# V and B of a hybrid decoder layer's input projection as a fourth seven-product pair

## The chip, the cores and the metric

One Trainium2 chip, one core. The metric is the device time of one execution in microseconds (us). TensorE multiplies, ScalarE (ACT) and VectorE (DVE) work on tiles, GpSimd (POOL) does elementwise work beside them, SyncE (SP) and ScalarE issue the transfers.

## The reference, cut to what matters

One layer (D = 1024) over a prompt of 1024 tokens and 8 sample rows, each sample with 4096 past positions in a paged K/V cache. Everything is float32.

```python
h = _rmsnorm(x, g_pre) * (1 + scale[:, None]) + shift[:, None]
p = h @ w_in                                   # 1024 x 4096
hc, bc, cc, gc, q, k, v, ga = jnp.split(p, _split_points(), axis=-1)   # 512 columns each
u = cc * hc
conv_y = sum(conv_w[i] * u_pad[:, i:i + L] for i in range(CONV_WIDTH))
ya = _rmsnorm(bc * conv_y, g_conv) * jax.nn.silu(gc)
o = attend(q, k, v, b_sb).reshape(Bsz, L, ATT_DIM)      # stick-breaking, strictly causal
yb = _rmsnorm(o, g_attn) * jax.nn.silu(ga)
m = jnp.concatenate([ya, yb], axis=-1) @ w_out
y = x + gate[:, None] * _rmsnorm(m, g_post)
# stick-breaking: z = q.k/sqrt(d) + b;  A[t,s] = exp(log_sigmoid(z_ts) + sum_{s<j<t} log_sigmoid(-z_tj))
```

Besides `y`, the outputs are K and V of the prompt (token by token) and of the samples, and the last rows of `u`.

## The kernel before, in words

**Prologue.** The modulation of the layer is computed from `w_ada`, x is normalised and transposed into `hT` (channels on partitions, 8 blocks of 128 channels by 1032 columns: 1024 tokens and 8 samples).

**Groups.** The 512 channels of each of the eight parts of the projection are worked in four groups of 128 channels, two heads each. A group runs through 32 slots `t` and an end. Slots 0 to 7 make Q, K and V; from slot 8 on each slot carries one of 24 attention units `u = t - 8` (`scores`, `clamp`, ScalarE's exponentials, `log_weights`, `turn`, `weights`, `outputs`), and between their steps TensorE works off products for the group's other parts (`pieces_at`). Every engine has its own program with the same slots, in an order written out by hand, and is held to the others by counted semaphores alone. A slot is thus no moment: SP and GpSimd run ahead of TensorE where they can.

**Beside it, the sample rows.** Per group there are two sequences of the sample batch. For each, K pages are loaded in 16 pairs into a ring of four (`load_pair`, SP), GpSimd multiplies a pair by the query (`prod`, two buffers), DVE reduces it (`reduce_pair`), and after two cumulated sums (`cumulate`, `decode_log_weights`) `decode_a` writes the weights into `apad`. V pages are loaded into a second ring and multiplied by TensorE (`value_quad`, eight quads per sequence).

**Seven products.** Two parts (for example Q and K) and the 1024 channels cut in halves make a 2x2 block product. It is done in seven products in place of eight, for chunks of 258 columns and their counterparts 516 columns on: `T1` to `T4` are sums of `hT`'s blocks (made once, DVE's `channel_sums`), `S1`, `S2`, `S4` and an overwritten `a21` are sums of the weight blocks, made by GpSimd in `weight_sum(g, pair, step)`, four steps. `product(i, j)` is product j of chunk i, four matmuls of 258 columns. ScalarE evacuates 1, 5, 6, 2, 4 (`evac_st`: a seed copy inside PSUM, `p5`, `u2`, then the two first outputs), DVE adds 3 and 7 (`product_sum`). Three pairs go this way: Q and K (not in group 0, where `project_qk` makes them directly), the gates GC and GA, and HC and CC.

**V and B.** V is made directly and by tokens (`values(0)`, `values(1)`, `values(2)` for the sample rows): `hT` is the stationary operand, 128 columns of the weight move. B is made directly in three thirds of 344 columns at the end of a group (`project_b`), before and between the last unit's steps. `gating` of a group runs on DVE in slots 0 to 6 of the next group: it multiplies the attention output and the convolution by their gates; in step 2 it takes the sample columns (a scan of two columns and five small copies) and multiplies `hcb` by B (`bcb`). Group 0 to 2 leave their two results in DRAM (`y_parts`).

**Output stage.** `y_parts` is loaded back (SP, after the last group's slots), w_out's eight 128-row slabs go into places that fall free (`wo`), and 16 units of 8 matmuls of 512 columns follow (`out_unit`), the first three in two parts round the last group's gating. Each unit goes through ScalarE and DVE and out.

In DVE's program `log_weights` is line 1239 and its subtraction line 1256, `reduce_pair` line 1226; GpSimd's page product is line 625 and `weight_sum` lines 594 to 608. All matmuls have line 1366 (`mm`), all of ScalarE's operations line 665 (`run`), K and V page loads line 394, w_out's line 400. The orders in question stand in two tables:

```python
EARLY = ((), (1, 5), (2, 6), (3, 7, 11), (4, 15), (12, 16), (13, 17))     # slot: (chunk, product) as two digits
GATING_AT = {0: 0, 1: 1, 2: 2, 4: 3, 5: 4, 6: 5}                          # slot: step
```

## Time and profile before

| | |
|---|---|
| median of 3 runs | 828.58 us (828.44 to 829.12) |
| the profiled execution | 826.34 us |
| its span, first to last instruction | 824.6 us |
| TensorE busy / mean granted clock | 785.9 us / 0.991 |
| DVE, ScalarE, GpSimd busy | 535.7, 352.1, 430.6 us |
| read from and written to HBM | 185 and 12 MB |

A float32 matmul appears in the trace as two records, so 8 records of 258 columns are one product. Matmuls are pipelined and the ends of their records are modelled: the price of a block is the distance from its start to the next block's start. Small transfers and waits that another engine covers cost nothing; what counts is where TensorE stands still.

### The profile page before, as it was taken

To read this page: it belongs to the slowest core of one execution; us is meant where nothing else is said; L and a number is where in the kernel's file an instruction comes from. 1 tells how busy PE (TensorE), PEld (TensorE's weight loads), DVE (VectorE), ACT (ScalarE), POOL (GpSimd) and SP (SyncE) were. 2 spreads that over 40 slices of the span, in tenths; PEclk is the share of its full clock that TensorE was granted. 3 is DMA by queue.
4 is the path that set the end of the run, shared out by engine and by line. 5 is a ranking of instruction groups with operands and counts; after the bars stand their busy time and mean duration, and the time that the engine had idled before them with its cause. 6 is when DMAs were issued, how large, how long until landed. Compare 5 with 4: busy or idle time off the path is not lost.

```text
span 824.6 us, 14401 instructions
## 1 busy us (share of the span) xinstructions
PE 785.9 (95%) x4397; PEld 523.3 (63%) x4397; DVE 535.7 (65%) x728; ACT 352.1 (43%) x729; POOL 430.6 (52%) x230
## 2 busy tenths in 40 slices
PE   0899989999999999999999999999999999999995
PEld 0455866676787676768866767788677665444442
DVE  3576769787585888838758877575787854232344
ACT  7301065775122667811165675122658731212122
POOL 0105895666787567666864685687666630100000
PEclk9989999999999999999999999999999999999998
DMA  8998667577689888776888877868977797554001
GB/s 318 362 348 291 223 225 227 187 240 234 229 260 306 286 255 263 249 248 219 279 290 262 269 238 230 255 234 290 307 253 243 220 360 276 167 188 157 27 27 53
DMA packets 131071, 197.85 MB, mean 240 GB/s; under 512 B 10025, under 2 KB 51030, under 8 KB 130994
## 3 DMA queue, kind: packets, MB, share of 16 engines
q1 hardware_dynamic: 99512, 181.11, 66.0%
q10 hardware_dynamic: 31482, 15.82, 6.9%
q8 instruction: 35, 0.57, 0.3%
q14 instruction: 42, 0.34, 0.2%
HBM read 185.25 MB, written 11.66 MB: 239 GB/s over the span
## 4 chain that ended last, share of the span: by engine, by line
PE 82%; DVE 6%; issue 4%; DMA 3%; POOL 3%; ACT 2%; SPq 1%; ACTq 0%; POOLq 0%; DVEq 0%
PE ps L1366 77%; PE ps L1606 4%; POOL prod L625 2%; DMA xT<-in_x_prompt_dram 2%; DMA ring<-in_w_in_dram 1%; DVE zd L1226 1%; DVE ps L1250 1%; DVE xT L1033 1%; DVE zc L1236 0%; DVE zc L1256 0%; PE ps L1408 0%; ACT tmp L665 0%; PE ps L1638 0%; DVE rows L1070 0%; DMA ring<-in_cache_v_dram 0%
## 5 line engine op out<-in xcount | busy, mean ns | idle before, releaser
L625 POOL TENSOR_TENSOR prod<-ring,qb 128x1024 f32<-128x1024 f32 x128 | 309.3, 2431 | 199.1 <-DVE zd L1226 96.8
L1366 PE MATMUL ps<-hT,wsl 128*128 128x258 f32 (+1 forms) x640 | 174.2, 418 | 0.2 <-DVE zb L1129 0.2
L1226 DVE TENSOR_REDUCE zd<-prod 128x16 f32<-128x1024 f32 x128 | 154.3, 1213 | 21.9 <-POOL prod L625 21.5
L1366 PEld LDWEIGHTS ps<-hT,wsl 128*128 128x128 f32 x640 | 119.1, 190 | 52.8 <-issue 17.3
L1366 PE MATMUL ps<-xT,wS 128*128 128x258 f32 x352 | 92.2, 385 | 0.0
L1366 PE MATMUL ps<-ring,apad 128*32 128x512 f32 x592 | 84.5, 650 | 7.9 <-DMA ring<-in_w_ada_dram 7.2
L1366 PE MATMUL ps<-xT,wsl 128*128 128x258 f32 x352 | 89.6, 386 | 0.0
L1250 DVE TENSOR_TENSOR_SCAN ps<-rise,ps 128x512 f32<-128x512 f32 (+3 forms) x64 | 65.5, 1023 | 34.0 <-ACT ps L665 34.0
L1236 DVE TENSOR_SCALAR zc<-ps,bsb 128x512 f32<-128x512 f32 (+3 forms) x96 | 54.8, 612 | 37.3 <-PE ps L1366 37.0
L665 ACT ACTIVATE rise<-ps,bsh 128x512 f32<-128x512 f32 (+3 forms) x96 | 55.4, 577 | 46.8 <-DVE zc L1236 46.7
L1366 PEld LDWEIGHTS ps<-xT,wsl 128*128 128x128 f32 x352 | 63.0, 190 | 18.6 <-issue 8.0
L665 ACT ACTIVATE av<-ps 128x512 f32<-128x512 f32 (+3 forms) x96 | 46.8, 487 | 60.1 <-PE ps L1606 59.4
L1366 PEld LDWEIGHTS ps<-xT,wS 128*128 128x128 f32 x352 | 62.3, 191 | 15.2 <-issue 8.7
L1366 PEld LDWEIGHTS ps<-wsl,hT 128*128 128x128 f32 (+1 forms) x576 | 63.3, 181 | 7.6 <-issue 6.4
L1366 PE MATMUL ps<-wsl,hT 128*128 128x128 f32 (+1 forms) x576 | 66.7, 276 | 0.6 <-ACT bcb L665 0.6
L1256 DVE TENSOR_TENSOR zc<-zc,ps 128x512 f32<-128x512 f32 (+3 forms) x96 | 52.9, 551 | 2.2
L658 POOL TENSOR_TENSOR rs<-ss,half 128x1 f32<-128x1 f32 x8 | 4.3, 543 | 90.8 <-DVE ss L1348 90.8
L1606 PE MATMUL ps<-ident,zc 128*128 128x128 f32 x288 | 47.6, 274 | 4.2 <-DVE zc L1256 4.1
L665 ACT ACTIVATE sp<-zc 128x512 f32<-128x512 f32 (+3 forms) x96 | 49.7, 517 | 0.0
L665 ACT ACTIVATE ps<-sp 128x512 f32<-128x512 f32 (+3 forms) x96 | 47.5, 495 | 3.0
L1366 PEld LDWEIGHTS ps<-av,vN 128*64 128x64 f32 x576 | 30.5, 136 | 27.6 <-issue 25.8
L1606 PEld LDWEIGHTS ps<-ident,zc 128*128 128x128 f32 x288 | 36.1, 141 | 16.5 <-DVE zc L1256 8.2
(241 smaller groups left out, 1013.9 us busy)
## 6 DMA issues: line engine op xcount, KB each, us to landing
ring<-in_cache_k_dram SPq DMA_DIRECT2D x256, 256.0 KB, 3.3
ring<-in_cache_v_dram SPq DMA_DIRECT2D x256, 256.0 KB, 3.0
wsl<-in_w_in_dram ACTq DMA_DIRECT2D x30, 512.0 KB, 6.2
ring<-in_w_ada_dram SPq DMA_DIRECT2D x5, 2048.0 KB, 14.5
xT<-in_x_prompt_dram SPq DMA_DIRECT2D x2, 2048.0 KB, 10.7
out_dram<-oT SPq DMA_DIRECT2D x8, 512.0 KB, 4.4
ring<-in_x_prompt_dram SPq DMA_DIRECT2D x8, 512.0 KB, 6.6
xT<-y_parts SPq DMA_DIRECT2D x6, 512.0 KB, 9.7
```

The lines of the kernel that those rows point to most:

```text
L625: pool.tensor_tensor(prod[:, p % 2].rearrange("p (j c) -> p j c", j=2), kring[:, p % 4], qb[:, p // 16].unsqueeze(1).to_broadcast([P, 2, H ...
L658: pool.tensor_tensor(rs[:, 20 + t % 2:21 + t % 2], ss[:, 20 + t % 2:21 + t % 2], half[:, 0:1], ALU.pow).then_inc(m_rstd, 1)
L665: nc.scalar.activation(out, in_, func, **kw).then_inc(done, 1)
L1033: v.tensor_scalar(xy[:, t, :], xy[:, t, :], rs[:, t:t + 1], None, ALU.mult).then_inc(x_scaled, 1)
L1226: v.tensor_reduce(zd[:, t // 16, :, r:r + 2], prod[:, t % 2].rearrange("p (j h d) -> p h j d", j=2, h=NH), AX_X, ALU.add)\
L1236: v.tensor_scalar(zc[:, u % 3, lo:QC], ps[:, Z + u % 3, 0:QC - lo], bsb[:, bass.ds(2 * g + h, 1)], CLAMP, ALU.add, ALU.min).then_inc(zc_re ...
L1250: v.tensor_tensor_scan(back(sums), back(rise[:, par_, lo + 1:QC + 1]), back(sums), start, ALU.add, ALU.add).then_inc(scan_done, 1)
L1256: v.tensor_tensor(zc[:, u % 3, lo:QC], zc[:, u % 3, lo:QC], sums, ALU.subtract)\
L1366: return nc.tensor.matmul(out, l, r, start=start, stop=stop, skip_group_check=True)
L1606: last = nc.tensor.transpose(ps[:, Z + u % 3, P * j:P * (j + 1)], zc[:, u % 3, lo + P * j:lo + P * (j + 1)], ident[:, :])
```

## The change

V and B become a fourth pair, number 1 of four, with chunks 2 and 3 of eight, in slabs 2 and 3 of the weight buffer. Their products are made in slots 0 to 7 and the next group's first four products (1, 5, 2, 6 of chunk 0) at the end of a group, where B was. The sums of the pair's weights are made by DVE (`value_weight_sum`), after the page sums of slots 2 and 3; those of Q and K, of which two were made in the next group's first slots, are made by GpSimd at the end of the group before, two of them ahead of the gate's product. V comes out channels first (`vT`, in the place of `av`) and is transposed by TensorE in two halves, in slots 7 and 9, through bank Z + 2. The sample columns are copied by ScalarE (`sample_columns`). In group 0 the second gate step comes in slot 6, behind the sums of V's first chunk; `gp` lies in `gab`. The last group has no next one: it starts the output projection with unit 2, k = 0 and 1. For that SP loads w_out's k = 0 in slot 26 and four parts in slots 30 and 31, the second branch's into the ring of K. The weights of the sample rows in `apad` are ordered from the end, so that a quad needs only the rows written, and are cleared once, before the fifth sequence.

The diff, cut to its core:

```diff
-SLABS = ((0, 1), (0, 3), (1, 2))
+SLABS = ((0, 1), (2, 3), (0, 1), (2, 3))
-EARLY = ((), (1, 5), (2, 6), (3, 7, 11), (4, 15), (12, 16), (13, 17))
+AHEAD = (1, 5, 2, 6)
+EARLY = ((3, 7, 11), (4, 15, 12, 16), (13, 17, 21), (14, 25, 22, 26), (23, 27, 31), (24, 35), (32, 36), (33, 37))
+EARLY_FIRST = {6: (21, 25, 22, 26, 23, 27, 31), 7: (24, 35, 32, 36, 33, 37)}
+TAKEN = {1: (4, 11, 15, 12, 16), 3: (14, 21, 25, 22, 26), 5: (24, 31, 35), 6: (32, 36)}
+TAKEN_FIRST = {6: (21, 25, 22, 26), 7: (24, 31, 35, 32, 36)}
+SUMMED = {1: 0, 3: 1, 5: 2, 8: 3}
+SUMMED_FIRST = {6: 2, 8: 3}
...
@@ SP
+                    if last and t == SLOTS - 1:
+                        for k in range(2):
+                            sp_e.wait_ge(prod_ready, 32 * GROUPS - 3 + k)
+                            load_part(1, k)
                     load_quad(g, first, t + 2)
...
+                    if last and t == SLOTS - 2:
+                        sp_e.wait_ge(part_out, 32 * (GROUPS - 1))
+                        sp_e.wait_ge(st_full[5], ALL)
+                        load_part(0, 0)
+                        load_part(0, 1)
+                    if last and t == 26:
+                        sp_e.wait_ge(st_full[2], CHUNKS * GROUPS - 4)
+                        load_wo(WO_ORDER[0])
+                        sp_e.wait_ge(st_full[4], CHUNKS * GROUPS - 4)
+                        load_wo(WO_ORDER[1])
...
             sp_e.wait_ge(z_full, NU * GROUPS)
-            load_wo(WO_ORDER[0])
-            load_wo(WO_ORDER[1])
-            sp_e.wait_ge(st_full[2], 6 * GROUPS - 2)
             load_wo(WO_ORDER[2])
             load_wo(WO_ORDER[3])
...
 # GpSimd, end of a group
+                if not last:
+                    weight_sum(g + 1, 0, 0)
+                    weight_sum(g + 1, 0, 1)
                 silu_mul(g, 1)
                 decode_scores(g, 1, first)
                 if not last:
-                    weight_sum(g + 1, 0, 0)
+                    weight_sum(g + 1, 0, 2)
                 decode_softplus(g, 1)
                 if not last:
-                    weight_sum(g + 1, 0, 1)
+                    weight_sum(g + 1, 0, 3)
...
 # ScalarE
                 if m == 0:
                     load_w(g, V_, 2)
+                    load_w(g, BC_, 3)
...
+            def value_rows_copy(g, first, c):
+                act.wait_ge(pj_full, PJ * g + c + 1)
+                if c == 0 and not first:
+                    act.wait_ge(vout, 16 * g)
+                run(vN[:, 4 * c:4 * (c + 1), :], ps[:, Z + 2, :].rearrange("p (t c) -> p t c", t=4), ACT.Copy, pj_free)
...
+            def sample_columns(g):
+                act.wait_ge(bconv_ready, g + 1)
+                part = lambda dst: dst[:, bass.ds(g, 1), :].rearrange("p a s -> p (a s)")
+                run(part(tail), ub[:, SEQ:SEQ + 2], ACT.Copy, sq_done)
+                for i, src in enumerate((ub[:, 2 + SEQ:2 + NT], bcb[:, SEQ:NT], gcb[:, SEQ:NT], gab[:, SEQ:NT])):
+                    run(part(samp[:, i]), src, ACT.Copy, sq_done)
...
-                evac_st(g, first, last, 5, 4)
-                evac_b(g, last, 0)
+                evac_st(g, CHUNKS - 1, 4)
+                for j in () if last else AHEAD[:2]:
+                    evac_st(g + 1, 0, j)
                 decode_logs(g, 1)
-                evac_b(g, last, 1)
-                evac_b(g, last, 2)
+                for j in () if last else AHEAD[2:]:
+                    evac_st(g + 1, 0, j)
                 decode_a(g, 1, first)
...
 # DVE
+            def value_weight_sum(g, step):
+                n = PAIRS * g
+                a11, a12 = wsl[:, 2, 0:4, :], wsl[:, 2, 4:8, :]
+                a21, a22 = wsl[:, 3, 0:4, :], wsl[:, 3, 4:8, :]
+                if step == 0:
+                    v.wait_ge(w_full[3], 16 * (2 * g + 1))
+                    v.wait_ge(q_out, 16)
+                    if n:
+                        v.wait_ge(st_full[5], 2 * n)
+                    v.tensor_tensor(S1, a21, a22, ALU.add).then_inc(vb_sum, 1)
+                if step == 1:
+                    ...
+                    if n:
+                        v.wait_ge(st_full[6], 2 * n)
+                    v.tensor_tensor(S2, S1, a11, ALU.subtract).then_inc(vb_sum, 1)
+                if step == 2:
+                    if n:
+                        v.wait_ge(st_full[3], 2 * n)
+                    v.wait_ge(vb_sum, 4 * g + 2)
+                    v.tensor_tensor(S4, a12, S2, ALU.subtract).then_inc(vb_sum, 1)
+                if step == 3:
+                    v.tensor_tensor(a21, a11, a21, ALU.subtract).then_inc(vb_sum, 1)
...
                     for p in sums_at(t):
                         reduce_pair(g, p)
+                    if t in (2, 3):
+                        value_weight_sum(g, 2 * (t - 2))
+                        value_weight_sum(g, 2 * (t - 2) + 1)
...
 # TensorE
+                def value_rows(c):
+                    if c == 0:
+                        pe.wait_ge(e_c11, CHUNKS * g + 2)
+                        if not first:
+                            pe.wait_ge(a_ready, NU * g)
+                    else:
+                        pe.wait_ge(d_c12, CHUNKS * g + 2)
+                        pe.wait_ge(pj_free, PJ * g + 1)
+                    for j in range(4):
+                        t = 4 * c + j
+                        last = nc.tensor.transpose(ps[:, Z + 2, P * j:P * (j + 1)], vT[:, P * t:P * (t + 1)], ident[:, :])
+                    last.then_inc(pj_full, 1)
...
+                    if u == 2:
+                        pe.wait_ge(pj_free, PJ * g + 2)
...
                     if u < NU:
                         for i, j, ks in pieces_at(u)[0]:
-                            product(i, j, ks)
+                            product(g, i, j, ks)
+                    elif last_:
+                        if u == NU:
+                            out_unit(2, (0, 1), True)
                     else:
-                        project_b(u - NU, range(0, 4))
+                        product(g + 1, 0, AHEAD[2 * (u - NU)])
                     if 1 <= u <= NU:
                         turn(u - 1)
                     if u == NU:
-                        product(5, 4)
+                        product(g, CHUNKS - 1, 4)
+                        if not last_:
+                            product(g + 1, 0, AHEAD[1])
...
                 outputs(NU - 2)
-                project_b(2)
+                if not last_:
+                    product(g + 1, 0, AHEAD[3])
                 cumulate(1)
```

## Rows read from the trace of the kernel before

**Rows 1.** The page: busy us by engine, and the chain that ended last.
```profile
PE 785.9 (95%) x4397; PEld 523.3 (63%) x4397; DVE 535.7 (65%) x728; ACT 352.1 (43%) x729; POOL 430.6 (52%) x230
...
PE 82%; DVE 6%; issue 4%; DMA 3%; POOL 3%; ACT 2%; SPq 1%; ACTq 0%; POOLq 0%; DVEq 0%
```

**Rows 2.** By stretch: PE, PEld, DVE, ACT, POOL busy us; clock; DMA share; GB/s.
```profile
106.00:216.00 110.00, 106.47 (x630) 73.55 (x630) 81.10 (x115) 67.26 (x143) 75.53 (x40) 1.00 0.72 228
216.00:261.00 45.00, 45.00 (x288) 38.04 (x288) 32.54 (x32) 7.94 (x18) 35.99 (x15) 1.00 0.79 250
261.00:672.00 411.00, 409.59 (x2525) 294.58 (x2529) 305.73 (x406) 216.63 (x457) 272.93 (x135) 1.00 0.82 261
672.00:684.00 12.00, 12.00 (x59) 7.56 (x60) 2.67 (x3) 2.52 (x7) 1.46 (x1) 1.00 1.03 406
684.00:700.00 16.00, 16.00 (x42) 7.35 (x40) 8.63 (x15) 2.92 (x5) 0.00 (x0) 1.00 0.67 265
```

**Rows 3.** Timeline of TensorE round group 1's start: start us, length us, what.
```profile
203.91 4.89 PE L1366 MATMUL ps<-hT,wsl 128*128 128x344 f32 x16
208.74 1.09 PE L1366 MATMUL ps<-av,vN 128*64 128x128 f32 x16
...
225.93 1.90 PE L1366 MATMUL ps<-xT,wS 128*128 128x258 f32 x8
227.67 1.90 PE L1366 MATMUL ps<-hT,wsl 128*128 128x258 f32 x8
...
249.21 7.41 PE L1366 MATMUL ps<-wsl,hT 128*128 128x128 f32 x64
256.46 1.91 PE L1366 MATMUL ps<-xT,wsl 128*128 128x258 f32 x8
258.30 1.91 PE L1366 MATMUL ps<-wsl,hT 128*8 128x128 f32 x16
260.14 0.66 PE L1638 MATMUL ps<-ident,kT 128*128 128x128 f32 x4
260.63 0.28 PE L1366 MATMUL ps<-ident_b,unseen 128*128 128x128 bf16 x2
```

**Rows 4.** Timeline of DVE in the same stretch: start us, length us, what.
```profile
220.12 2.54 DVE L1184 SCALAR_TENSOR_TENSOR gab<-oT,par,gab 128x1024 f32<-128x1024 f32 x1
...
226.05 1.16 DVE L1187 TENSOR_TENSOR_SCAN last<-naught,ub 128x2 f32<-128x2 f32 x1
227.25 2.29 DVE L1190 COPY tail<-last 128x2 f32<-128x2 f32 x1
```

**Rows 5.** Groups of instructions: count, busy us, mean ns of one, idle before.
```profile
L625 POOL TENSOR_TENSOR prod<-ring,qb 128x1024 f32<-128x1024 f32 x128 | 309.3, 2431 | 199.1 <-DVE zd L1226 96.8
...
L1256 DVE TENSOR_TENSOR zc<-zc,ps 128x512 f32<-128x512 f32 x48 | 32.7, 681 | 0.5
...
L665 ACT ACTIVATE rows<-ps 8x128 f32<-8x128 f32 x8 | 2.1, 266 | 6.8 <-PE ps L1366 6.0 <-PE ps L1641 0.8
```

**Rows 6.** TensorE's waits between 98 and 216 us: total us, times, longest.
```profile
PE ps L1606 <- DVE zc L1256: 3.1, 4, 1.3
```

**Rows 7.** The last group's end: ScalarE, GpSimd, SP by time; DMA sizes and landing.
```profile
672.33 0.41 ACT L665 ACTIVATE om<-zb 128x256 f32<-128x256 f32 x1
...
672.94 0.85 ACT L665 ACTIVATE om<-om 128x256 f32<-128x256 f32 x2
...
673.87 1.46 POOL L568 TENSOR_TENSOR spd<-spd,om 128x256 f32<-128x256 f32 x1 [7.12 <-ACT om L665]
...
661.91 0.43 SPq L400 DMA_DIRECT2D qT<-in_w_out_dram  x1
...
xT<-y_parts SPq DMA_DIRECT2D x6, 512.0 KB, 9.7
...
qT<-in_w_out_dram SPq DMA_DIRECT2D x1, 512.0 KB, 6.1
...
rise<-in_w_out_dram SPq DMA_DIRECT2D x1, 512.0 KB, 11.6
```

More of the change, by code:

```diff
@@ L59 @@
 SLOTS = 32
+SQUARES = 7
 LAG_FROM = 10
@@ L65 @@
 PART = [4, 5, 6, 3, 7, 0, 2, 1]
-PJ = 6
+PJ = 2
 MS = 5
@@ L775, in evac_st @@
                 if j == 1:
-                    if not (first and i == 2):
+                    if n:
                         act.wait_ge(e_c21, n)
```

494 lines of the change are left out of this document (228 added, 266 removed).

## The prediction

> **What bounds the kernel now.** I read the page's head and its chain of waits first. TensorE is busy 785.9 us, 95% of the span, and 82% of the chain that ended last is TensorE [rows 1]. The table by stage then shows where it is not: it loses 3.5 us of the 110 us that hold group 0's attention, none in the 45 us before group 1's attention, 1.4 us in the next 411 us and none in the last group's end [rows 2]. So from 47 us on nearly every microsecond of TensorE is a microsecond of the kernel, and the change is a change of TensorE's work. The question is only whether the other engines still deliver in time.
>
> **What is removed.** The timeline of TensorE at the end of group 0 and the start of group 1 gives the prices, from start to start [rows 3]. Four blocks of V by tokens (32 matmuls of 128 columns) take 256.46 - 249.21 = 7.25 us, and there are two. V's eight sample rows take 260.14 - 258.30 = 1.84. A third of B takes 8 matmuls of 344 columns, 208.74 - 203.91 = 4.83 us, and there are three. Together 14.5 + 1.84 + 14.5 = 30.8 us per group, 123.3 in four.
>
> **What is added.** Seven products for each of two column chunks. A product (4 matmuls of 258 columns) takes 227.67 - 225.93 = 1.74 us, fourteen take 24.4. V comes out transposed now, so it needs 8 transposes of 128x128 and one for the sample columns; four such transposes of K take 260.63 - 260.14 = 0.49 us [rows 3], nine take 1.1. Together 25.5 us per group, 102.0 in four. The balance is **-21.3 us**, group 0 included: its Q and K stay as they are, its V and B change like the others.
>
> **Where the work lies.** Three things move. (1) The end of a group held 14.5 us of B; it now holds four products of the next group's Q and K, 7.0 us. (2) The stretch before the attention held V and fourteen products; it now holds 24 products, three page-value quads, four V and four K transposes. 24 x 1.74 is 41.8, with 3.2 for the quads and 1.0 for the transposes 46.0 us, against 45 now [rows 2]. (3) Group 0 starts its attention later and gets that back at its end.
>
> **Is the cover at a group's end enough?** The last unit's weights need ScalarE's exponential after TensorE's turn; between the turn and the outputs there are now two products, a quad and a third product (6.3 us), where ScalarE needs under a second for a copy and one exponential. The product's seed copy waits behind the last evacuation, which has a product and a quad over it. Softplus of the second sequence needs ScalarE's four short operations, 672.33 to 673.79 in the last group, and GpSimd's sum [rows 7]; another product lies over that. GpSimd makes the next group's first two sums before its gate product, so page scores come later by two sums, some 3 us, inside an idle time of 7.1 us that the softplus has [rows 7]. Cost taken: nothing for groups 0 to 2.
>
> **The stretch before the attention, DVE's queue.** It gains four V sums (two SBUF inputs, 128x512), four product sums more (about 0.42 us each), and loses the scan and five small copies. No row has the V sum. The nearest form on DVE, one input in PSUM, takes 0.68 us [rows 5]: the lower bound. The upper comes from what two-column operations show there: the scan took 1.16 us and the copy of two columns 2.29 us while GpSimd was inside a page product, and a 1024-column operation 2.54 us [rows 4]. So a V sum can cost 0.68 + 2.43 = 3.1 us, the second term a whole page product [rows 5]. I take a value nearer the lower end, 1.65, since GpSimd's two product buffers stand full part of the time: 4 x 1.65 = 6.6 us, of which the removed scan and copies give back 4.1 (1.16, 2.29 and four of about 0.16). Setting the order out by hand, DVE ends the second product sum of chunk 1 about 0.8 us before TensorE's product 4 of that chunk asks for it, chunk 2's 1.2 us before, and is free 2 to 3 us before the first scores. Behind the V sum that waits for TensorE (S2 needs chunk 1's product 6) stand the convolution's product, the product sums and the K reductions; behind those GpSimd's page products, then SP's K loads. All of it has the 46 us to catch up. Taken at nothing; bounds 0 and 3.3 us per group (rival 1).
> The Trainium skill (SBUF — State Buffer, section "Who interferes with whom") says that a VectorE instruction with two SBUF inputs and a GpSimd instruction that reads SBUF exclude each other for their whole length. The trace agrees: 2.29 us for two columns. By that rule taken at its worst, every V sum costs 3.1 us; the sum would lose the 3.3 us in each of three groups.
>
> **ScalarE** gets ten evacuations of chunks per group for six, and the sample copies. Nearest row for an 8-column copy: 0.27 us for 8 partitions, PSUM source [rows 5]; between DVE's 0.16 and that, five make at most 1.4 us, in a stretch where ScalarE worked 7.9 of 45 us [rows 2]. Free. One place costs: the second copy of V's rows (0.6 us) now stands before the third score may be written, behind the first unit's exponential, with half a product (0.87 us) over 1.2 us: 0.3 us per group, **+1.2**; bounds 0 and 0.6 each. The clears of the weight matrix go from one before each sequence to three before the fifth: under 1 us, once, hidden. SP's store of V waits some 8 us longer and holds K and V loads behind it; K is loaded four pairs ahead, so nothing.
>
> **Group 0.** The 3.5 us that TensorE loses there are turns that wait for DVE (3.1 us) [rows 6], because GpSimd's page products started late. The attention now starts 7.9 us later on TensorE's clock while DVE and GpSimd are held only about 3 us, by the chunk's sums and the second gate step behind them. I take **-2.3**; bounds -3.5 and +1. B's weights go out at ScalarE's first evacuation instead of in mid-attention, and the V sums come after the first reductions; both are in place before TensorE's product 5. The fetch of the query rows has 512 KB more before it, 1.3 us at 406 GB/s [rows 2], under DVE's first gate step.
>
> **Last group.** No next group stands behind it: four matmuls of the output projection fill in (3.4 us) and the other 12.0 us of the first three units come after. The fill needs w_out's rows for k = 1, which SP still issues at 661.91, after all scores, one behind the other; the first landed after 6.1 us [rows 7], so 668, the second some 1.3 us later, while TensorE asks at 664.9 + 1.7 = 666.6. Ahead of them are now four parts of 512 KB (9.7 us to landing [rows 7]), but these start from 653.6 on, and the queues moved 406 GB/s when full [rows 2]: done at about 662. Wait 2.0 us, before the last turn. Then the softplus has only product 4, a quad and the outputs over it and comes 1.4 us late. **+3.4**; bounds 0 and 9. DVE's decode sums and gating, 8.6 us of work right behind the cumulated sums (684 to 700) [rows 2], fit under the 12.0 us. SP's earlier loads of two slabs of w_out (in slot 26) meet queues with room, and cost nothing.
>
> **Sum.** -21.3 + 1.2 - 2.3 + 3.4 = **-19.0 us** against the profiled execution's 826.3 (span 824.6 and 1.7 around it), which gives 807.3. That execution is 2.2 us under the median of the three runs, 828.6; on the median the forecast is **809.6 us**.
>
> **Rivals.**
> 1. *DVE's sums come late* (chance 0.14). For: the margin at chunk 1 is 0.8 us and DVE's operations doubled beside GpSimd's [rows 4]. Against: DVE idles in this stretch now (32.5 of 45 us busy [rows 2]). If the two V sums before that point cost 3.1 instead of 1.65 each and the convolution's product 1.2 more, TensorE waits 4.1 - 0.8 = 3.3 us in three groups: +9.9, 819.5.
> 2. *The last group's fill waits longer* (0.12). Parts and w_out share the queues; w_out to `rise` took 11.6 us [rows 7]. At that landing TensorE waits 6 to 7 instead of 2: 814 to 815.
> 3. *Slower than before* (0.04): DVE and GpSimd go strictly in turns before the attention, and this becomes the bound. 13 reductions at GpSimd's 2.43 us, four V sums at 3.1, about 16 us of gating, decode and product sums are 60 us against TensorE's 46: 14 us in three groups, +43, 852. It decides from 52.3 us on, where three stretches eat the 19. Against: DVE's 32.5 and GpSimd's 36.0 busy us in those 45 [rows 2] overlap for at least 23.5.
> 4. *The change does not save what it says* (0.04): a product takes longer in the mixed order or the waits before each of the 24 products leave gaps of 0.2 us. 24 x 0.2 x 4 = 19: no change. Against: fourteen such products stand gapless in group 1 [rows 2].
> My forecast, with its own range of 804 to 813, has 0.66.
>
> **Range.** Down to 828.6 - 21.3 - 3.5 = 803.8 with no new wait at all; up to 819.5 with rival 1. A measurement here can tell about 0.2%, 1.7 us: faster 0.94, same 0.02, slower 0.04.
>
> **What would show it.** Right: groups of V (128x128, hT moving from wsl) and of 344 columns from B gone, 448 more records of 258 columns; TensorE's idle in the three stretches before the attention under 1 us; an idle of about 2 us before the matmuls out<-qT,xT in the last group, with w_out named, and one of 1.4 before the cumulated sums; DVE's V sums at 0.7 to 3 us. Wrong: TensorE waiting for DVE's kT or bcb sums (rival 1); V sums of 3.1 us all and reductions behind GpSimd (rival 3); product starts over 1.8 us apart (rival 4).

## The result and the profile after

The changed kernel takes **813.44 us** (median of 4 runs, 811.55 to 815.84); the kernel before, run beside it, 828.69 (828.44 to 829.12). The ratio is 0.9823, with a 95% interval from 0.98 to 0.9845: 15.3 us less, where 19.0 were forecast, and 3.8 us above the predicted 809.6. The profiled execution was the longest of the four, 815.84 us with a span of 814.1. So the same kernel was run again later; its profiled execution took 812.41 (span 810.7), and is called "the repeat" below. Where one execution could mislead, both stand. One execution of the split fill below took 3254 us and is left out of its figures. The measured time lies inside the stated range (803.8 to 819.5) and 0.4 us above the narrower one, 804 to 813, that the prediction gave its own forecast.

The head of the page of the kernel after, to be held against [rows 1]:

```profile
PE 772.0 (95%) x4113; PEld 510.9 (63%) x4113; DVE 566.4 (70%) x735; ACT 361.2 (44%) x769; POOL 432.7 (53%) x230
...
PE 75%; DVE 8%; issue 5%; DMA 4%; SPq 4%; POOL 2%; ACT 1%; POOLq 0%; DVEq 0%; ACTq 0%
```

TensorE has 284 matmul records fewer and is still the bound, but the chain of waits now has more than work in it. The table by stretch (length, TensorE, weight loads, VectorE, ScalarE, GpSimd busy; clock; DMA share; GB/s) says where; it answers to [rows 2]:

```profile
118.00:218.00 100.00, 98.11 (x611) 69.67 (x608) 80.52 (x114) 67.32 (x143) 68.69 (x37) 1.00 0.71 229
219.00:266.00 47.00, 47.00 (x230) 38.01 (x230) 39.35 (x34) 9.62 (x25) 37.50 (x16) 1.00 0.89 285
266.00:660.00 394.00, 392.50 (x2356) 281.19 (x2354) 315.39 (x407) 220.51 (x475) 270.97 (x134) 1.00 0.84 268
660.00:676.00 16.00, 11.26 (x48) 5.79 (x44) 3.63 (x5) 2.32 (x6) 5.84 (x4) 0.79 1.03 406
676.00:689.00 13.00, 12.51 (x31) 6.00 (x32) 10.86 (x11) 3.02 (x8) 0.39 (x1) 1.00 0.71 265
```

The stretch before the attention of group 1 holds 47.0 us of TensorE in 47.0, as worked out (46). In the 394 us that follow it misses 1.5 us. The trouble is in one place, 660 to 676: 4.7 us without work, and a clock of 0.79. TensorE's timeline of that place (start us, length us, what, the idle time before it in brackets):

```profile
661.16 1.10 PE L1440 MATMUL ps<-wsl,xT 128*128 128x512 f32 x2 [0.96 <-DMA ring<-y_parts]
662.10 1.02 PE L1440 MATMUL ps<-wsl,ring 128*128 128x512 f32 x2
666.27 2.07 PE L1440 MATMUL ps<-qT,xT 128*128 128x512 f32 x2 [3.15 <-DMA qT<-in_w_out_dram]
668.13 1.92 PE L1440 MATMUL ps<-kT,ring 128*128 128x512 f32 x2
669.84 1.06 PE L1601 MATMUL ps<-ident,zc 128*128 128x128 f32 x4
670.69 2.63 PE L1440 MATMUL ps<-xT,wsl 128*128 128x258 f32 x8
...
676.49 0.67 PE L1440 MATMUL ps<-spd,ntri 128*128 128x256 f32 x2 [1.12 <-issue]
```

The predicted wait for w_out is there, 3.15 us and not 2.0. Behind it stands what the prediction has no term for: the two matmuls of the fill that take 1.02 us each elsewhere take 2.07 and 1.92, the turn 1.06 for about 0.60. The table by stretch of TensorE alone (length, busy; clock; DMA share; GB/s) gives the reason; its clock fell to the lower of its two levels (0.50, 1.2 GHz) while the engine stood for w_out:

```profile
664.00:668.00 4.00, 1.73 (x2) 0.67 1.02 412
668.00:672.00 4.00, 4.00 (x11) 0.50 1.02 416
672.00:676.00 4.00, 3.37 (x30) 0.98 1.04 399
```

**The account by stages**, from starts of TensorE's matmuls in three traces: the first V work of group 0, the cumulated sums behind each group (ps<-spd,ntri), and the statistics (ps<-ones,ssa). Differences to before in us; the forecast column spreads the prediction's -19.0 over the same stages.

| stage | before | after | repeat | forecast |
|---|---|---|---|---|
| to the first V work | 86.47 | +2.3 | +1.7 | 0 |
| group 0 | 128.02 | +1.5 | +0.6 | -0.4 |
| group 1 | 156.05 | -5.1 | -5.1 | -5.0 |
| group 2 | 156.93 | -5.3 | -3.8 | -5.0 |
| group 3 | 156.03 | -0.4 | -2.7 | -5.2 |
| first units behind it | 16.31 | -3.4 | -3.4 | -3.4 |
| the rest | 124.79 | -0.1 | -1.2 | 0 |
| span | 824.6 | -10.5 | -13.9 | -19.0 |

The trade of products for plain matmuls pays to a tenth of a us where it stands alone, in group 1. The loss is in group 3, with a smaller one in group 0. The first row I take for an effect of the execution and not of the change, though no run shows it. From 40 to 60 us TensorE's mean clock was 0.74 in the profile of after, for 0.83 before; in the repeat it was 0.83 too, but TensorE waited 2.34 us for a transfer instead of 1.60. The last 48 records of 344 columns ahead of the V work then take 13.97 us in all three. In the profiles of the other versions, with the prologue of the changed kernel, the V work began 0.4 to 2.5 us behind 86.47 (86.83 to 88.93). The one profile of before began it earlier than all thirteen others, which fits the 2.2 us that the prediction added between that execution and the median; there is no profile of a longer execution of before to show it.

### The profile page after: what moved, and what is told of

Read it like the earlier page. It is cut to its first block, busy times and chain, and to the rows that moved or that the text cites. A ratio compares the mean times of both kernels' runs of the same rounds, so it can differ in the third digit from the quotient of the medians.

```text
span 814.1 us, 13946 instructions
## 1 busy us (share of the span) xinstructions
PE 772.0 (95%) x4113; PEld 510.9 (63%) x4113; DVE 566.4 (70%) x735; ACT 361.2 (44%) x769; POOL 432.7 (53%) x230
## 4 chain that ended last, share of the span: by engine, by line
PE 75%; DVE 8%; issue 5%; DMA 4%; SPq 4%; POOL 2%; ACT 1%; POOLq 0%; DVEq 0%; ACTq 0%
PE ps L1440 70%; PE ps L1601 3%; DMA ring<-in_w_ada_dram 3%; POOL prod L665 2%; SPq L420 2%; DVE zd L1300 1%; SPq L412 1%; DVE ps L1324 1%; PE ps L1482 1%; DMA qT<-in_w_out_dram 1%; DVE zc L1310 1%; DVE wS L1157 0%; PE ps L1633 0%; PE ps L1543 0%; DVE zc L1330 0%
## 5 line engine op out<-in xcount | busy, mean ns | idle before, releaser
L1440 PE MATMUL ps<-hT,wsl 128*128 128x258 f32 (+1 forms) x576 | 145.8, 397 | 0.3 <-DVE zb L1205 0.3
L1440 PEld LDWEIGHTS ps<-hT,wsl 128*128 128x128 f32 x576 | 107.7, 191 | 33.4 <-issue 12.2
L1440 PE MATMUL ps<-xT,wS 128*128 128x258 f32 x480 | 122.9, 385 | 0.0
L1440 PE MATMUL ps<-xT,wsl 128*128 128x258 f32 x480 | 121.6, 388 | 0.7 <-DVE bcb L1186 0.6
L1440 PEld LDWEIGHTS ps<-xT,wsl 128*128 128x128 f32 x480 | 87.5, 191 | 27.2 <-issue 10.8
L1440 PEld LDWEIGHTS ps<-xT,wS 128*128 128x128 f32 x480 | 86.2, 190 | 20.0 <-issue 10.1
L1440 PE MATMUL ps<-ring,apad 128*32 128x512 f32 (+3 forms) x592 | 84.0, 648 | 7.8 <-DMA ring<-in_w_ada_dram 6.8
L708 ACT ACTIVATE av<-ps 128x512 f32<-128x512 f32 (+4 forms) x104 | 49.9, 480 | 76.7 <-PE ps L1601 63.4
L1440 PE MATMUL ps<-hT,wS 128*128 128x258 f32 x240 | 62.3, 391 | 0.0
L1440 PEld LDWEIGHTS ps<-hT,wS 128*128 128x128 f32 x240 | 42.5, 190 | 19.1 <-issue 14.7
```

The costliest lines, as they stand in the source:

```text
L708: nc.scalar.activation(out, in_, func, **kw).then_inc(done, 1)
L1440: return nc.tensor.matmul(out, l, r, start=start, stop=stop, skip_group_check=True)
```

## Experiments

Twelve runs, each with five or six executions beside the kernel before. The repeat and the first three versions ran on one chip (before there 827.45), the other eight on another, at two times (before 827.6 and 827.2). Times are thus compared on one chip, across chips the ratios to the kernel before.

**The changed kernel again** (no edit).

> The changed kernel again, unchanged, as the yardstick of this chip. My theory: the executions differ by how long TensorE's clock stands at half in two places, the prologue and the 3.15 us wait of the last group; so the median lies at 813.4 as before, single times between 811 and 816, and the mean clock goes with them (0.992 to 0.984). Rival: the spread has another source; then times and clock do not go together.

Measured: 812.26 us (811.64 to 812.41), ratio 0.981 [0.9795, 0.9824]. Its waits show the last group's fault again (columns: who waited for whom, us in total, times, longest):

```profile
PE ps L1440 <- DMA qT<-in_w_out_dram: 3.2, 1, 3.2
...
PE ps L1440 <- issue: 2.2, 2, 1.1
```

The wait for w_out is a property of the change (3.2 us again); the 0.6 us wait for VectorE's bcb in group 0 is not there every time. The five times lie within 0.8 us of each other, too close to test the expectation about the spread.

### The last group's fill

**No fill**: all twelve matmuls of the first units behind the cumulated sums.

```
                     elif last_:
-                        if u == NU:
-                            out_unit(2, (0, 1), True)
+                        pass
...
-            out_unit(2, (2,))
+            out_unit(2, range(GROUPS - 1), True)
```

> No matmuls of the output projection before the last turn; the first three units come whole behind the cumulated sums. Theory (the fill costs more than it covers: 0.96 us for a part, 3.15 us for w_out, then about 3 us of half clock): turn at 660.2 on the profile's clock of the changed kernel, cumulated sums at about 668.3 instead of 677.4, then 3.4 us more of units: 5 to 6 us faster, 808. No stretch of half clock in the last group. Rival (the fill is needed as cover, and what is lost there is the softplus's latency): the idle before the cumulated sums grows by the 3.4 us that the fill worked, and the time stays within 1 us of the changed kernel.

Measured: 810.05 us (807.92 to 810.64), ratio 0.9782 [0.9765, 0.98]: **2.2 us less than the repeat, with the cover taken away**. TensorE's waits between 650 and 686 us of this version:

```profile
PE ps L1440 <- DMA ring<-in_cache_v_dram: 2.7, 1, 2.7
PE ps L1440 <- DMA rise<-in_w_out_dram: 1.6, 1, 1.6
```

A fill that must wait is worse than none. But other things then stand bare: TensorE asks for the last quad's V pages at 660.1 and has them at 662.8, and w_out's later rows cost 1.6 us. So the gain is neither the 5 to 6 us of the theory nor the nothing of the rival.

**Split fill**: k = 0 stays before the last turn, k = 1 goes behind the last outputs, where the softplus is waited for.

```
                         if u == NU:
-                            out_unit(2, (0, 1), True)
+                            out_unit(2, (0,), True)
...
                 if not last_:
                     product(g + 1, 0, AHEAD[3])
+                else:
+                    out_unit(2, (1,), True)
                 cumulate(1)
```

> Only k = 0 of the fill before the last turn, k = 1 between the last outputs and the cumulated sums, when w_out has landed. Theory: the wait of 3.15 us and the half clock behind it go, the 0.96 us for the part stays: 6 to 7.5 us faster than the changed kernel, 806 to 807.5. Rival (softplus's latency): w_out's wait turns into a wait before the cumulated sums; at most 1 us faster.

Measured: 808.11 us (805.39 to 808.74), ratio 0.9749 [0.973, 0.9768], 4.2 us less than the repeat, where 6 to 7.5 were expected. The fill's second half comes at 665.75 with no wait for w_out, and the 1.12 us before the cumulated sums are gone too, since the fill lies over the softplus. This version's timeline:

```profile
659.65 1.10 PE L1440 MATMUL ps<-wsl,xT 128*128 128x512 f32 x2 [0.84 <-DMA ring<-y_parts]
...
665.75 1.12 PE L1440 MATMUL ps<-qT,xT 128*128 128x512 f32 x2
666.72 1.02 PE L1440 MATMUL ps<-kT,ring 128*128 128x512 f32 x2
667.57 0.59 PE L1440 MATMUL ps<-spd,ntri 128*128 128x256 f32 x2
```

**Early w_out**: the fill as in the change, but SP asks for its rows ahead of the last V pages.

```
                             load_part(1, k)
+                        sp_e.wait_ge(z_full, NU * GROUPS)
+                        load_wo(WO_ORDER[2])
+                        load_wo(WO_ORDER[3])
...
-            sp_e.wait_ge(z_full, NU * GROUPS)
-            load_wo(WO_ORDER[2])
-            load_wo(WO_ORDER[3])
```

> The order of TensorE is unchanged; SP issues w_out's two slabs for k = 1 right after the last K pages instead of after the last V pages, ahead of the two parts of the second branch. Theory (the wait is for w_out because SP gets to it late, behind a V load that waits for a quad): no wait for w_out, but the parts behind it come up to 2.4 us later, so the first wait grows from 1 to about 3 us: 1 to 4 us faster, 809 to 812. Rival (the queues are full, whatever the order): the wait only changes its name, and the time stays within 1 us.

Measured: 808.31 us (807.32 to 810.36), ratio 0.9768 [0.975, 0.9785], 4.0 us less than the repeat. Same order of work on TensorE, only the data earlier. Its waits between 650 and 686 us:

```profile
PE ps L1440 <- issue: 1.1, 1, 1.1
PE ps L1440 <- DMA ring<-y_parts: 0.7, 1, 0.7
PE ps L1440 <- DMA qT<-in_w_out_dram: 0.5, 1, 0.5
PE ps L1440 <- DMA kT<-in_w_out_dram: 0.2, 1, 0.2
```

SP now issues these loads at 653.10 and 653.76 instead of 658.18 and 658.66 in the repeat, and the clock stays at 1.00 from 660 to 672. By the stages of the two profiles, group 3 is 3.2 us shorter than in the repeat (150.2 for 153.4). From the first matmul of the fill to the cumulated sums it is 3.7 us, of which 2.6 are the wait for w_out (3.24 to 0.67) and the rest most of the clock's share; the parts of y, now behind w_out, take back 0.5 (a wait of 0.72 for 0.17). The clock's share is read from start to start behind the wait: the first pair of matmuls 1.86 for 0.97 us, the second 1.36 for 0.86, 1.4 us in the repeat; in the profile of after it goes on over the turn and the product (1.86, 1.71, 0.85, 2.57 for 0.97, 0.86, 0.44, 1.84), 2.9 us. Outside group 3 the two profiles differ by -1.0 us ahead of the V work, +1.2 in group 0, -1.2 in group 2 and +0.8 behind the first units, where the edit changes nothing; that is the spread of single profiles, and the medians carry the 4.0. Two different edits, one on TensorE and one on SP, take the wait away and bring 4 us each: the wait, with what hangs on it, is the cause of the loss in group 3.

**Fill behind**: k = 0 behind the last product, over ScalarE's exponential, k = 1 behind the last outputs.

```
                     elif last_:
-                        if u == NU:
-                            out_unit(2, (0, 1), True)
+                        pass
...
                         product(g, CHUNKS - 1, 4)
                         if not last_:
                             product(g + 1, 0, AHEAD[1])
+                        else:
+                            out_unit(2, (0,), True)
...
+                else:
+                    out_unit(2, (1,), True)
                 cumulate(1)
```

> The changed kernel with the last group's fill moved: the four matmuls of k=0 not before the last turn but behind the last product, over ScalarE's exponential, and those of k=1 behind the last outputs, over the softplus. The first w_out rows are asked for 2.6 us later and the turn never stands behind them. The version with k=0 before the turn and k=1 behind the outputs took 4.15 us less than the changed kernel. Theory (the 3.15 us wait for w_out and the half clock behind it, some 3 us, are the last group's excess): no wait for w_out over 0.5 us, the clock stays up, 807 to 808.5, at or up to 1 us under the version with k=0 before the turn. Rival (the turn and scores, not covered by the four matmuls, then wait for V's pages or for ScalarE, as in the version with no fill, 2.65 us): 809.5 to 811.

Measured: 807.8 us (806.71 to 808.95), ratio 0.9755 [0.9738, 0.9771]; and once more, later:

> The version with the last group's fill behind the last product and behind the last outputs once more, beside the version that also has the sums on GpSimd, so that the two are compared on one chip. Expected as measured before: ratio 0.974 to 0.977, 806.5 to 808.5 us, no wait for w_out over 0.5 us in the last group and TensorE's clock up from the last products to the cumulated sums. If it comes out above 809.5, the 4.5 us gained by the place of the fill were partly the luck of that chip.

Measured: 805.8 us (804.65 to 809.47), ratio 0.9754 [0.9731, 0.9778]. It cannot be told from the split fill. In the first profile no wait over 0.25 us is left between 650 and 680, in the second one of 0.86 for w_out's later rows. Group 3 is 5.1 us shorter than in the repeat, and 1.8 us were gained ahead of it, where the edit does nothing: the cumulated sums start at 667.26 for 674.20. Of these 6.9 us 4.6 arrive at the end of the span. The timeline of TensorE behind the output units, in this version,

```profile
682.34 2.93 PE L1440 MATMUL ps<-ones,ssb 128*128 128x1 f32 x16
685.20 3.61 PE L1440 MATMUL ps<-ring,apad 128*8 128x512 f32 x16
688.74 4.24 PE L1440 MATMUL ps<-hT,xT 128*128 128x512 f32 x8
```

and in the repeat

```profile
688.86 1.93 PE L1440 MATMUL ps<-ones,ssb 128*128 128x1 f32 x16
690.71 1.92 PE L1440 MATMUL ps<-ring,apad 128*8 128x512 f32 x16
692.56 3.70 PE L1440 MATMUL ps<-hT,xT 128*128 128x512 f32 x8
...
697.80 1.06 PE L1440 MATMUL ps<-ring,apad 128*8 128x512 f32 x8 [1.55 <-DMA ring<-in_cache_v_dram]
```

shows where it goes: behind the one-column sums the clock falls in the faster version (0.50 from 683.5 to 689.5), the three groups of matmuls take 3.2 us longer, and 1.3 us of a wait for V pages vanish in exchange. The repeat's trace has no fall there; those of before and after have a shorter one.

### VectorE, GpSimd and ScalarE before the attention

**Sums on GpSimd**: the four V/B weight sums issued by GpSimd in the same slots.

```
 # VectorE
-                    if t in (2, 3):
-                        value_weight_sum(g, 2 * (t - 2))
-                        value_weight_sum(g, 2 * (t - 2) + 1)
...
 # GpSimd, value_weight_sum with pool in place of v
+                    if t in (2, 3):
+                        value_weight_sum(g, 2 * (t - 2))
+                        value_weight_sum(g, 2 * (t - 2) + 1)
                     if t == 10:
                         decode_scores(g, 0, first)
```

> The changed kernel with the four V/B weight sums per group issued by GpSimd (ahead of its other work of slots 2 and 3) instead of VectorE; same operands, same results. In the changed kernel a sum takes VectorE 1.70 to 2.84 us, and TensorE has no idle time in the stretches before the attention of groups 1 to 3. Theory (the sums lie under cover wherever they stand, VectorE's slack was enough): same time as the changed kernel within 1 us, 811 to 813.5; VectorE's busy time falls by about 37 us (16 sums of 2.3), GpSimd's rises by more than that, its page products come later, TensorE loses at most 0.5 us per group. Rival (the two engines share one budget before the attention, and GpSimd's page products are its tight part): GpSimd needs a third product's time per sum (2.4 to 5 us each, 10 to 20 us per group), K reductions come late, TensorE waits for DVE's kT or zc by 2 us or more in each group: 818 or more.

Measured: 813.78 us (810.33 to 815.4), ratio 0.9824 [0.9801, 0.9846]: the same as the changed kernel. In its trace TensorE is busy for 142.0 of 142.0 us in the three stretches before the attention. The rival is out. What a sum costs depends on the engine. The groups of the kernel after (VectorE; busy us, mean ns of one):

```profile
L1164 DVE TENSOR_TENSOR wsl<-wsl 128x512 f32<-128x512 f32 x4 | 11.4, 2839 | 0.0
L1157 DVE TENSOR_TENSOR wS<-wS,wsl 128x512 f32<-128x512 f32 x4 | 10.7, 2670 | 0.4
L1162 DVE TENSOR_TENSOR wS<-wsl,wS 128x512 f32<-128x512 f32 x4 | 8.0, 2002 | 0.0
L1151 DVE TENSOR_TENSOR wS<-wsl 128x512 f32<-128x512 f32 x4 | 6.8, 1692 | 0.0
```

and of this version (GpSimd):

```profile
L668 POOL TENSOR_TENSOR wS<-wS,wsl 128x512 f32<-128x512 f32 x4 | 5.1, 1270 | 0.5
```

Sixteen sums occupy VectorE for 36.9 us, 2.31 each, and GpSimd for 20.4, 1.28 each: on GpSimd's own queue they stand between its page products and not beside them. The expectation had GpSimd's busy time grow by more than VectorE's falls, and it grew by less. The edit also gives the stretch a margin that the changed kernel has not. TensorE's product 4 of chunk 1 asks for VectorE's last sum of that chunk (kT). In this version the sum is done 1.11 us before the product starts, and the product starts 1.74 us behind the one before it, its plain price (a line of VectorE, a line of TensorE):

```profile
233.60 0.43 DVE L1189 TENSOR_TENSOR kT<-ps,stage 128x258 f32<-128x258 f32 x1 [1.26 <-PE ps L1440]
...
235.14 1.90 PE L1440 MATMUL ps<-xT,wsl 128*128 128x258 f32 x8
```

**Sums made twice**: VectorE's first two sums of each group are issued a second time.

```
+                    v.tensor_tensor(S1, a21, a22, ALU.add).then_inc(dbl, 1)
+                    v.wait_ge(dbl, 2 * g + 1)
                     v.tensor_tensor(S1, a21, a22, ALU.add).then_inc(vb_sum, 1)
...
+                    v.tensor_tensor(S2, S1, a11, ALU.subtract).then_inc(dbl, 1)
+                    v.wait_ge(dbl, 2 * g + 2)
                     v.tensor_tensor(S2, S1, a11, ALU.subtract).then_inc(vb_sum, 1)
```

> The changed kernel with VectorE's first two V/B weight sums of each group made twice, one behind the other (1.70 + 2.67 = 4.4 us more per group, same values). It measures how much room VectorE has before TensorE's fifth product of the second column chunk, where the changed kernel's trace shows VectorE's product sum done at 237.75 and that product starting at 237.80. Theory (there is no room left beyond 0.1 us; rival 1 of the prediction stood just behind the door): TensorE waits 3.5 to 4.4 us for VectorE's kT or bcb sum in each of groups 1 to 3 and in group 0: 826 to 830. Rival (TensorE does not ask for that sum until later, so several us are free): less than 1.5 us per group, under 818.

Measured: 817.31 us (814.36 to 819.97), ratio 0.987 [0.9848, 0.9892]: against the ratios of the changed kernel (0.9823 and 0.981) 0.5 to 0.6% or 4 to 5 us more, between the two expectations. TensorE's waits in its trace:

```profile
PE ps L1444 <- DVE kT L1190: 4.4, 3, 1.6
...
PE ps L1444 <- DVE bcb L1190: 1.7, 1, 1.7
```

The timelines of group 1 say why it is not 4.4 per group. The kernel after, VectorE and, in the last two lines, TensorE:

```profile
231.37 1.70 DVE L1151 TENSOR_TENSOR wS<-wsl 128x512 f32<-128x512 f32 x1
233.15 2.67 DVE L1157 TENSOR_TENSOR wS<-wS,wsl 128x512 f32<-128x512 f32 x1
...
237.33 0.42 DVE L1186 TENSOR_TENSOR kT<-ps,stage 128x258 f32<-128x258 f32 x1
...
236.04 1.90 PE L1440 MATMUL ps<-hT,wsl 128*128 128x258 f32 x8
237.80 2.01 PE L1440 MATMUL ps<-xT,wsl 128*128 128x258 f32 x8
```

This version, in the same order:

```profile
234.18 2.73 DVE L1153 TENSOR_TENSOR wS<-wsl 128x512 f32<-128x512 f32 x1
237.00 0.69 DVE L1159 TENSOR_TENSOR wS<-wS,wsl 128x512 f32<-128x512 f32 x1
237.72 0.69 DVE L1161 TENSOR_TENSOR wS<-wS,wsl 128x512 f32<-128x512 f32 x1
...
237.12 1.90 PE L1444 MATMUL ps<-hT,wsl 128*128 128x258 f32 x8
240.39 2.01 PE L1444 MATMUL ps<-xT,wsl 128*128 128x258 f32 x8 [1.36 <-DVE kT L1190]
```

Four sums take 5.80 us where two took 4.37. Whichever comes second stands behind GpSimd's page product (2.67 or 2.73); those after it find GpSimd idle and take 0.69, the lower bound of the prediction. From the first sum to the operation behind the sums VectorE needs 5.88 us for 4.38, 1.50 more, and the product starts 3.27 us behind the one before it for 1.76, 1.51 more. So **there is no margin at chunk 1**. The trace of after says so too, though it counts no wait there, since the ends of matmul records are modelled: in groups 1, 2 and 3 the product starts 0.05 us behind the end of the kT sum, as it does here after a wait, and 1.76, 1.79 and 2.03 us behind the product before it, for a price of 1.74. The changed kernel loses 0.02, 0.05 and 0.29 us at this place. My expectation had 0.1 us of room, and the price of a repeated sum too high.

**Sample columns by VectorE**: five small copies per group back on VectorE, ScalarE's squares at their old place.

```
-SQUARES = 7
+SQUARES = 2
...
-                            sample_columns(g - 1)
...
 # VectorE, ahead of the convolution's product
+                    v.tensor_copy(part(tail), ub[:, SEQ:SEQ + 2])
+                    for i, src in enumerate((ub[:, 2 + SEQ:2 + NT], bcb[:, SEQ:NT], gcb[:, SEQ:NT], gab[:, SEQ:NT])):
+                        v.tensor_copy(part(samp[:, i]), src)
```

> The changed kernel with the sample columns copied by VectorE again (five copies of 2 or 8 columns per group, from the same buffers) and ScalarE's squares at their old place. Theory (ScalarE's copies bought VectorE time that it did not need in groups 1 to 3): VectorE's busy time grows by some 12 us (per group 2.3 for a copy that falls into a GpSimd product and four of about 0.16, more if more of them fall into one), the total stays within 1 us of the changed kernel, 811 to 813.5. Rival (the copies stand in VectorE's queue just before the convolution's product on which B's product sums, K reductions and the next page products hang): TensorE waits for VectorE by 1 to 2 us per group, 815 to 819.

Measured: 814.76 us (810.74 to 817.66), ratio 0.983 [0.9805, 0.9854]: no different from the changed kernel within the interval. The copies take 0.16 us each and overlap; from the first to the next operation is 0.36 us, and there are no 2.3 us for one of them. Without a margin these 0.36 us are lost in full: TensorE's product starts 2.12, 2.14 and 2.39 us behind the one before it, 0.35 to 0.36 more than in the kernel after in each group. The times are too wide to show these 1.1 us; the traces do. The 2.29 us that such a copy took before [rows 4] was no price of the copy but of the page product beside it; here none falls into one.

**Second gate step early**: back at the end of slot 5.

```
-                    if first and t == 6:
-                        gates(1)
...
-                    if first and t == 0:
-                        gates(0)
+                    if first and t in (0, 5):
+                        gates(t // 5)
```

> The changed kernel with only the second gate step put back where it stood (VectorE, end of slot 5 of group 0, before the V additions of slot 6). It says whether putting it behind V's addition bought anything. In group 0 of the changed kernel TensorE loses 0.6 us (for VectorE's bcb) just before the attention and 1.9 us within it. Theory (group 0 kept a stall because VectorE and GpSimd are held by these steps): the early gate step delays V's row additions by its 2.6 us, and the bcb wait grows from 0.6 to 2 or 3 us: 813.5 to 815. Rival (the step's place does nothing; either order is covered): within 0.7 us of the changed kernel. A second rival: page products start earlier because the gates are there earlier, the 1.9 us within the attention goes, and the time falls by 1 us or more.

Measured: **819.71 us** (818.64 to 824.03), ratio 0.9909 [0.9888, 0.9931], 1% above the changed kernel and more than any expectation had. TensorE's timeline in group 0 and, from the table by stretch, its clock:

```profile
100.87 1.90 PE L1438 MATMUL ps<-hT,wsl 128*128 128x258 f32 x8
109.24 3.81 PE L1438 MATMUL ps<-xT,wsl 128*128 128x258 f32 x8 [6.46 <-DVE bcb L1186]
112.83 2.98 PE L1438 MATMUL ps<-xT,wS 128*128 128x258 f32 x8
```

```profile
109.00:112.00 3.00, 2.76 (x7) 0.50 0.57 175
112.00:116.00 4.00, 4.00 (x13) 0.62 0.00 0
```

The clock is at its lower level from 108.5 to 115.0; it fell while TensorE stood. The gate step's five operations hold VectorE from 102.88 to 108.4, ahead of V's row sum (108.42 here, 103.47 in the kernel after). TensorE waits 6.46 us instead of 0.62, and the two products behind it take 2.8 us more, nearly all of it at half clock: 8.7 us from the first V work to the first scores (37.55 for 28.88). The ratios show 0.9 to 1.0% of 828, 7 to 8 us. The least conspicuous part of the change is worth half of what the whole brings.

**GpSimd's old order** at a group's end: gate product and page scores ahead of the next group's first two sums.

```
-                if not last:
-                    weight_sum(g + 1, 0, 0)
-                    weight_sum(g + 1, 0, 1)
                 silu_mul(g, 1)
                 decode_scores(g, 1, first)
+                if not last:
+                    weight_sum(g + 1, 0, 0)
+                    weight_sum(g + 1, 0, 1)
```

> The changed kernel with GpSimd's order at a group's end put back: its second gate product and the scores of the next pages ahead of the next group's first two weight sums. The changed kernel shows no TensorE wait for GpSimd's sums or for the softplus chain in groups 1 and 2. Theory (the new order was needed for the sums, because the next group's products now start before the group's end): products 0 to 3 of the next group wait for the sums, 1 to 4 us in each of the three transitions, 815 to 824. Rival (the sums are early enough in either order, and the scores come 2.6 us earlier): within 1 us of the changed kernel, 811 to 813.5.

Measured: 813.39 us (811.75 to 813.72), ratio 0.9827 [0.9811, 0.9842]: no difference. The order was free either way.

**Fill behind, sums on GpSimd**: both edits.

> The changed kernel with the last group's fill behind the last product and behind the last outputs, and the V/B weight sums on GpSimd. Alone the first took 807.8 us against 827.6 for the kernel before (ratio 0.9755); the second 813.8 (0.9824), in its profiled execution without the 0.6 us wait for VectorE's bcb and the 1.4 us wait for hT ahead of group 0's attention. Theory (the weight sums are covered on either engine, only group 0's wait goes): 0.3 to 1.5 us under the fill alone, ratio 0.974 to 0.9752. Rival (GpSimd's page products, 5 us later per group, meet the last group's chain): 0.5 us or more above it.

Measured: 807.77 us (806.37 to 809.43), ratio 0.9767 [0.9749, 0.9786], against 0.9754 [0.9731, 0.9778] for the fill alone beside it. The sums' place adds nothing that the times can tell, and decides between neither expectation; in this trace too the kT sum is done 1.11 us ahead of its product in each of the three groups. The version to keep is the changed kernel with the fill behind (or split): 0.975 of the time before, 20 us, where the change as made gets 15.

## Why the prediction was right, and where it was off

- **What bounds the kernel, and the balance per group (-21.3)**: right. Group 1 lost 5.1 us for 5.0 forecast, in both executions. Products start 1.74 us apart (229.08, 230.82, 232.56 in group 1). No run tried it alone; it is read from the traces. Rival 4 is out.
- **The stretch before the attention taken at nothing**: right in the total, wrong in the margin. The V sums take 2.31 us on average instead of the 1.65 taken (1.70 + 2.67 before chunk 1 instead of 3.3). That uses up the 0.8 us of margin that was worked out and leaves none. Rival 1 came by 0.02 to 0.29 us per group instead of 3.3, 0.4 us in all, and the doubled sums and the sample copies show how near it was: each further microsecond on VectorE there is one of the kernel's. That the total held was in part luck, since the value of 1.65 was a choice between bounds and no row had the sum. Rival 3 would have needed this to hold for the whole stretch; with 39.4 us of VectorE in 47, it does not. The Trainium skill (SBUF — State Buffer, section "Who interferes with whom") says that a VectorE instruction with two SBUF inputs contends with a GpSimd instruction that reads SBUF, for ports held as an exclusive lock: 2.67 against 0.69 us for the same operation agrees with it. The row that the prediction held against this rule, 2.29 us [rows 4], is of a copy with one SBUF input, which that sentence does not cover; the scan ahead of it has two, and took 1.16 for 0.16 in the last group, where GpSimd is idle. The consequence taken at the worst (3.1 us each) was too much: the means of the four sums lie from 1.69 to 2.84.
- **ScalarE (+1.2)**: free where it was called free; the sample copies take 0.20 us. The one place with a price was put too high: in groups 1 to 3 the third scores start 0.06 us behind ScalarE's copy of V's rows and 1.02 us behind the half product before them, for 0.87, so 0.15 us per group and not 0.3.
- **Group 0 (-2.3, so that the stage comes to -0.4)**: off by 1.0 us in the repeat, 1.9 in the profile of after. The waits that I expected to go mostly stayed: 1.9 us of idle from 118 to 218 and 0.6 before the scores, for 3.5 us before, so about 1.0 us and not 2.3. Two early turns still wait for VectorE (0.5 and 0.9 us). I had put V's row sums and the gate step in one line, as "held only about 3 us". Had the step stayed where it was, this stage would have cost 8 us more; the prediction took the move into account but never priced it.
- **Last group (+3.4)**: the term that was mis-sized. Group 3 came out 2.5 us over the forecast of its stage in the repeat and 4.8 in the profile of after, so the term measured 5.9 to 8.2. It has two parts. The stalls: w_out's rows came at 666.3 and TensorE had asked at 663.1, where the prediction had them at 668 and some 1.3 us later and TensorE's asking at 666.6; both were earlier, TensorE by more, and it waited 3.15 for 2.0. With 0.96 for the parts of y and 1.12 before the cumulated sums that is 5.2 us for 3.4. And the clock, 1.4 us in the repeat and 2.9 in the profile of after, which the sum did not hold at all: a wait was priced at its length alone. Rival 2 had named the place and, with 814 to 815, nearly the total, but by a wait of 6 to 7 us that did not come. Against the profile of before the repeat misses the forecast by 5.1 us: 2.5 by this term, 1.0 in group 0, 1.2 in group 2 and 1.7 ahead of the V work, less 1.2 behind the first units. The median missed by 3.8; medians have no stages, so its parts can't be told.
- **Execution against median (+2.2)**: not shown either way. The later medians of before are 827.2 to 827.6, 0.9 to 1.2 us above the profiled execution, on other chips or at other times.

What stays open: why the units' data come so late. Through 660 to 676 the queues moved 399 to 416 GB/s with a share of 1.0, so the loads ask for more than they get; which of them could move out of this stretch was tried for w_out's first two slabs only. The 1.5 us by which group 2 of the repeat is slower than that of after (1.04 of them an idle time before cumulated sums within the group, named "issue") were not looked into.

## What to carry to other kernels

A stall of some microseconds on a busy TensorE costs more than its length: here 3.2 us brought 1.4 to 2.9 us of half clock with them and 6.5 us brought 2.8, while 2.6 us brought none, so a sum should hold both. Work that fills a gap must have its operands by then; if it waits for a transfer, put it one gap later or ask for the transfer earlier: either brought 4 us. Read a margin from start to start, not from the waits alone: this trace counts no wait at a place where the margin is zero. And price every step that is moved on an engine's queue, even the one that looks like tidying: the second gate step was worth 8 us, and by the traces the place of the sample copies 1.1, that of the weight sums 0.4.

## What was not expected of the hardware

- TensorE's clock fell to the lower level while the engine stood 3.15 us for w_out (and 3.24 in the repeat, 6.46 with the early gate step), or, in four other versions, up to 1.4 us after such a wait (2.70 us with the sums on GpSimd, 2.92 with the doubled sums, 3.11 with GpSimd's old order, 3.21 with the sample columns by VectorE). It was back 3 to 7 us later. It did not fall at waits of 0.84 us (split fill), 2.59 us (w_out, early gate step) and 2.65 us (no fill; granted clock 1.00 from 656 to 672).
- It also fell with TensorE without a gap, at or behind 16 matmuls of one column each (32 records, ones,ssa and ones,ssb), for some 3 to 7 us, in twelve of the fourteen traces, those of before and after among them; in the repeat and with the early gate step not at all.
- The same 128x512 sum of two SBUF operands takes VectorE 0.69, 1.69, 2.00, 2.67 or 2.84 us, and GpSimd, in the same slots, 1.26 to 1.30. Elsewhere in that trace GpSimd's sums take as much, but for some of one form (up to 2.25).
